# Layer 0's mixer in three-pass products: heads, gaps and forward heads on other engines, another order of products

## What is computed

```python
hl = modulate(x_lat, norm_g[l, 0], mod_l[0], mod_l[1])   # rms norm, gain, shift
hc = modulate(x_ctx, norm_g[l, 0], mod_c[0], mod_c[1])
aq, ak, av, ao, ag, bq, bk, bv = split_cols(h @ w_in, EVEN_SPLITS)
# mLSTM, 4 heads of 128, forward and backward in time:
dmat = where(tri, b[t] - b[s] + li[s], -inf);  m_t = maximum(inter, max(dmat))
w = exp(dmat - m_t);  s = (q @ k.T) * w
h = num / maximum(abs(den), exp(-m_t))            # forward h + backward h
mlstm = sigmoid(ao) * rms_norm(h, head_g)
# window attention, 8 heads of 64, 2 key heads, rope, a sink per head, over context and band
lat = concatenate([mlstm, b_lat]);  x = x + mod[2] * (lat @ w_out)
```

## Time and profile before

| | |
|---|---|
| median of 3 runs | 1662.94 us |
| the profiled execution, its span | 1663.01 us, 1661.7 us |
| PE busy | 1559.9 us, 94% |
| PEld, DVE, ACT, POOL busy | 78%, 70%, 44%, 29% |
| chain that ended last | PE 81%, DVE 9%, ACT 5% |
| heads of layer 0 (131.29 to 298.38) | 55.58, 55.58 and 55.93 us |
| head 0 ends | 131.29 us |

### The profile page before, as it was taken

How to read it: one execution, slowest core, us unless ns; L and a number is a source line. 1 busy time by engine, 2 the same in 40 slices (tenths; PEclk the granted TensorE clock), 3 DMA queues, 4 the chain that set the end, 5 groups by cost and what they waited for, 6 DMA issues and landing times.

```text
span 1661.7 us, 25035 instructions
## 1 busy us (share of the span) xinstructions
PE 1559.9 (94%) x9548; PEld 1298.8 (78%) x9548; DVE 1155.7 (70%) x2094; ACT 723.8 (44%) x1349; POOL 481.1 (29%) x385
## 2 busy tenths in 40 slices
PE   6999999989999999989898999998999999999888
PEld 5565566768888888866667999998888888898778
DVE  5467787869777797747767788666666666543764
ACT  2442434353333333344442655544444444454454
POOL 1012104102221110115430111025566656532652
PEclk9999999999999999999999999999999999999999
DMA  9223224314344466503234555553444434444240
GB/s 389 104 102 125 91 64 140 140 38 167 138 152 152 141 209 204 193 20 102 94 109 166 178 184 184 186 174 115 144 143 137 137 136 133 136 134 148 88 143 26
DMA packets 63943, 231.23 MB, mean 139 GB/s; under 512 B 7520, under 2 KB 8544, under 8 KB 63568
## 3 DMA queue, kind: packets, MB, share of 16 engines
q1 hardware_dynamic: 60912, 218.66, 38.7%
q0 software_dynamic: 2192, 6.29, 1.1%
q10 hardware_dynamic: 720, 4.68, 0.7%
HBM read 228.55 MB, written 1.05 MB: 138 GB/s over the span
## 4 chain that ended last, share of the span: by engine, by line
PE 81%; DVE 9%; ACT 5%; issue 3%; DMA 1%; POOL 1%; SPq 0%; ACTq 0%; DVEq 0%; POOLq 0%
PE ps L267 13%; PE ps L269 13%; PE ps L268 13%; PE ps L249 10%; PE ps L1314 4%; PE ps L1316 4%; PE ps L1315 4%; PE ps L257 2%; PE ps L742 2%; PE ps L732 2%; DVE big L687 2%; PE ps L635 1%; ACT big L668 1%; DMA ring<-in_ada_first 1%; DVE weights_rest L282 1%
## 5 line engine op out<-in xcount | busy, mean ns | idle before, releaser
L282 DVE TENSOR_TENSOR weights_rest<-ring,weights_rounded 128x1024 fp32r<-128x1024 f32 x192 | 267.4, 1394 | 69.8 <-ACT weights_rounded L276 69.5
L276 ACT ACTIVATE weights_rounded<-ring 128x1024 fp32r<-128x1024 f32 x233 | 244.3, 1053 | 119.7 <-PE ps L1316 94.1
L267 PE MATMUL ps<-h_hi,weights_rounded 128*128 128x512 f32 (+1 forms) x640 | 215.0, 336 | 0.0
L268 PE MATMUL ps<-h_lo,weights_rounded 128*128 128x512 f32 (+1 forms) x640 | 215.0, 336 | 0.0
L269 PE MATMUL ps<-h_hi,weights_rest 128*128 128x512 f32 (+1 forms) x640 | 215.0, 336 | 0.0
L1300 POOL TENSOR_TENSOR big<-scratch 128x512 f32<-128x512 f32 (+1 forms) x44 | 64.2, 1460 | 392.2 <-DVE scratch L1286 392.2
L288 POOL TENSOR_TENSOR weights_rest<-ring,weights_rounded 128x1024 fp32r<-128x1024 f32 x41 | 98.4, 2404 | 177.3 <-ACT weights_rounded L276 177.3
L1240 ACT ACTIVATE scratch<-ps,vectors 128x512 f32<-128x512 f32 (+1 forms) x88 | 59.1, 672 | 191.0 <-PE ps L269 182.2
L249 PE MATMUL ps<-h,ring 128*128 128x512 f32 x288 | 132.6, 617 | 2.2 <-DVE h L488 2.2
L269 PEld LDWEIGHTS ps<-h_hi,weights_rest 128*128 128x128 f32 x640 | 121.5, 190 | 12.6
L268 PEld LDWEIGHTS ps<-h_lo,weights_rounded 128*128 128x128 f32 x640 | 121.5, 190 | 12.5
(11 more groups left out here) (383 smaller groups left out, 3979.2 us busy)
## 6 DMA issues: line engine op xcount, KB each, us to landing
ring<-in_up SPq DMA_DIRECT2D x88, 512.0 KB, 3.8
ring<-in_ada_rest SPq DMA_DIRECT2D x80, 512.0 KB, 4.5
ring<-in_a_in SPq DMA_DIRECT2D x80, 512.0 KB, 3.5
ring<-in_down SPq DMA_DIRECT2D x44, 512.0 KB, 3.6
ring<-in_even SPq DMA_DIRECT2D x20, 512.0 KB, 4.2
ring<-in_ada_first SPq DMA_DIRECT2D x16, 512.0 KB, 9.0
ring<-in_wout SPq DMA_DIRECT2D x16, 512.0 KB, 3.6
ring<-in_odd SPq DMA_DIRECT2D x16, 512.0 KB, 3.7
```

What stands on the lines that cost most here:

```text
L267: te.matmul(bank[:, 0:n], wh[:, k, :], hi(k), start=k == 0, stop=False)
L268: te.matmul(bank[:, 0:n], wh[:, k, :], lo(k), start=False, stop=False)
L276: sc.activation(pair[0], place(*key), ACT.Copy).then_inc(*mark("rounded", *key))
L282: ve.tensor_tensor(pair[1], place(*key), pair[0].bitcast(F32), ALU.subtract).then_inc(*mark("rest", *key))
```

## The change

- The five products of each head and the three of even_pre are `pe_product3` products. ACT rounds each tile; the rests of tiles 0, 1 and 4 (of head 0 also 2) and of even_pre 1 and 2 are on POOL, the others on DVE. The tiles are released at the rest instead of the product. The output projection's first pairs continue the rotation of the slots.
- h is split: DVE scales 16 half blocks, ACT adds the shift and rounds, DVE subtracts. The three tiles of even_pre are rounded before the fourth group of rows is copied; the rows are turned between the products of ada_first; gates' and keys' products run block by block together, ahead of the values'.
- The values' products have the model dimension on the partitions; ACT copies them, TensorE transposes four blocks, ACT copies again.
- The gaps are on ACT, straight from the spread maxima in PSUM (Relu, bias, then Exp); MREP and its copies are gone. Each head's two spreads stand at the end of the head before, those of head 0 behind its product 2. GT holds the negative.
- The forward heads are on ACT (a copy with a scale from PSUM).
- DVE's adaptive tiles stand elsewhere in a head; in head 0 five of them stand between rope and decays. One tile moves from layer 1's heads to layer 1's output projection.

```diff
     for i in range(AH):
-        tile(("even", i, 0), "even", 5 * i, "product", "even", i, 0)
+        for s in range(3):
+            tile(("even", i, s), "even", 5 * i + s, even_rest(i, s), "even", i, s)
         ada_tiles(6 * i + 4, 6 * i + 5, 6 * i, 6 * i + 1)
...
-    ODD_ADA = [(68, 69), (70, 71), (72,), (73,)]
+    ODD_ADA = [(68, 69), (70,), (71,), (72,)]
+    WOUT1_ADA = [(73, 74), (75,), (76,), (77,), (78,), (79,), (), ()]
...
             if g == 3:
                 act_rsqrt((0, 0), TOK)
+                for x in range(3):
+                    act_round(("even_pre", x), PAIR_PRE[x], [])
...
+            if s in (8, 12, 15):
+                pe_rows(s // 4 - 2 + (s == 15))
...
+        for x, (k, s, cols) in enumerate(parts):
+            ve.scalar_tensor_tensor(FULL_EVEN[:, cols], xv[:, k, 256 * s:256 * s + 256], GAIN[:, s * KD + k:s * KD + k + 1],
+                                    RS[:, 256 * s:256 * s + 256], ALU.mult, ALU.mult).then_inc(*mark("scaled", "even", k, s))
+            if x >= 2:
+                rest(*parts[x - 2])
...
+    def pe_spread(i):
+
+        for dr in range(2):
+            te.wait_ge(*at("maxima", dr))
+            te.matmul(BANK[SPREAD[dr]], CT[0:4, C_SEL + 128 * i:C_SEL + 128 * i + 128], rows[6 + dr], start=True,
+                      stop=True).then_inc(*mark("maxima_spread", dr, i))
...
     def pe_even(i):
         us, E = sum(units0(i), []), ("even", i)
-        pe_product(("even", i, 0), BANK[6], TOK, hk(0, TOK))
+        pe_even_product(i, 0, BANK[6])
+        if i == 0:
+            pe_norm(KEY0, t1, BANK[1], TOK)
+            pe_even_turn(("even_pre", 2), VFM0[0], BANK[2])
+        pe_even_product(i, 1, BANK[7])
+        if i:
+            te.wait_ge(*at("mixed_heads", i - 1))
+        pe_norm(("even", i, 0), t1, BANK[5], TOK)
+        te.wait_ge(*at("aq_copied", i))
+        pe_even_product(i, 2, BANK[7])
         if i == 0:
             pe_gates()
...
+            te.wait_ge(*at("v_copied", 0))
             pe_spread(0)
...
+        te.wait_ge(*at("gaps", i, 0, *last_gap(0)))
...
-        pe_product(("even", i, 4), BANK[7], TOK, hk(0, TOK))
+        pe_even_turn(("even", i, 3), VFM0[1], BANK[6])
+        pe_even_product(i, 4, BANK[7])
...
+        if i + 1 < AH:
+            pe_spread(i + 1)
         te.wait_ge(*at("heads_normed", i))
...
         def gap_exps():
+            sc.wait_ge(*(at("numerators", i - 1, 3) if i else at("gates_copied")))
+            for dr, s, lo, n, pos, W in decays():
+                sc.wait_ge(*at("maxima_spread", dr, i))
+                c = 128 * s + 64 * dr + i
+                sc.activation(W, BANK[SPREAD[dr]][:, lo:lo + n], ACT.Relu,
+                              bias=GT[:, c:c + 1]).then_inc(*mark("gaps", i, dr, s, lo))
...
         sc.wait_ge(*at("product", "even", i, 3))
+        sc.wait_ge(*at("normed", "even", i, 0))
+        sc.activation(VFM0[1], BANK[6], ACT.Copy).then_inc(*mark("copied", "even", i, 3))
+        act_even_round(i + 1, 0)
+        sc.wait_ge(*at("turned", "even", i, 3))
         sc.activation(av3[:, :, 0:128], v3(BANK[6], 128), ACT.Copy).then_inc(*mark("av_copied", i))
...
         act_exps(us)
+        act_even_round(i + 1, 1)
         sc.wait_ge(*at("product", "even", i, 4))
...
+            if t:
+                forward_head(t - 1)
+        forward_head(3)
...
         dve_rope(E, ROPE1, BANK[5], t2, [] if i else [at("roped", *KEY0)])
-        dve_ada(6 * i + 2)
+        if i == 0:
+            ve.wait_ge(*at("cond_rows_act"))
+            dve_ada(4)
+            dve_ada(0)
+            dve_ada(2, 1)
...
+        pool_even_rest(i, 4)
+        pool_even_rest(i + 1, 0)
+        pool_even_rest(i + 1, 1)
```

More of the change, by code:

```diff
@@ L493, in build, with even_parts, act_even_h @@
-    K0, V0, MREP = BIG[:, 0:512], BIG[:, 512:1024], BIG[:, 1024:5120]
+    H_HI0, H_LO0 = rounded("h_even_hi", "h", 0, KD * TOK), rounded("h_even_lo", "big", 1024, KD * TOK)
+    FULL_EVEN = MIX
+    def even_parts():
+        for k in range(KD):
+            for s in range(2):
+                yield k, s, slice(k * TOK + 256 * s, k * TOK + 256 * s + 256)
+    def act_even_h():
+        for k, s, cols in even_parts():
+            sc.wait_ge(*at("scaled", "even", k, s))
+            sc.activation(H_HI0[:, cols], FULL_EVEN[:, cols], ACT.Identity,
+                          bias=mod(0, 0, s)[:, k:k + 1]).then_inc(*mark("h_rounded", "even", k, s))
+            if (k, s) == (4, 1):
+                act_even_round(0, 0)
+        act_even_round(0, 1)
@@ L494, in build @@
+    K0, V0 = BIG[:, 0:512], BIG[:, 512:1024]
     arow = BIG[:, 6144:6144 + 5120]
     rows = [arow[0:4, TOK * j:TOK * j + TOK] for j in (2, 3, 4, 5, 6, 7, 0, 1, 8, 9)]
+    rows[6:8] = [RS[0:4, TOK * j:TOK * j + TOK] for j in range(2)]
     GT, EM, MASK0 = SCR[:, 0:512], SCR[:, 512:544], SCR[:, 544:1568]
@@ L540, in act_pre @@
         act_square(KEY0, t1, BANK[0], TOK)
+        sc.wait_ge(*at("product", "even_pre", 2))
+        sc.activation(VFM0[0], BANK[2], ACT.Copy).then_inc(*mark("copied", "even_pre", 2))
+        act_even_round(0, 2)
         act_norm(KEY0, t1, BANK[1], TOK)
-        sc.wait_ge(*at("product", "even_pre", 2))
+        sc.wait_ge(*at("turned", "even_pre", 2))
         sc.activation(V0, BANK[2], ACT.Copy).then_inc(*mark("v_copied", 0))
-    def act_maxima(dr):
-        for h in range(AH):
-            x = AH * dr + h
-            sc.wait_ge(*at("maxima_spread", dr, h))
-            sc.activation(MREP[:, x * TOK:(x + 1) * TOK], BANK[SPREAD[x % 3]],
-                          ACT.Copy).then_inc(*mark("maxima_copied", dr, h))
     def act_floors():
@@ L604, in pool_pre @@
     def pool_pre():
+        for x in (1, 2):
+            pool_rest(("even_pre", x), PAIR_PRE[x], [])
         po.wait_ge(*at("square_sum", "x", KD - 1))
```

235 lines of the change are left out of this document (120 added, 115 removed).

## The result

The changed kernel took 1668.4 us, median of 14 runs, against 1663.0 for the kernel before on the same chip: ratio 1.0028, 95% interval 1.0019 to 1.0038. It is slower by 0.3%, where 1646.9 was forecast and 1654.5 was the range's upper end. The profiled execution has a span of 1666.5 us, which with 1.3 around it is 1667.8.

The account below looks back on a forecast made before the run. TensorE bounds a head up to S, an ACT and DVE chain its tail. Head 0 -1.7, heads 1 and 2 -8.4, head 3 -5.0, odd heads -2.4, projection +0.2, contention +1.2: -16.1, 1663.0 to 1646.9; range 1640 to 1654.5.

Parts of the forecast that it names:

- Products of 5.44, S 29 after the start: Layer 0's heads: three-pass products take 5.44 us; S, the end of attention scores, comes 6.0 earlier, 29.0 after head start.
- The tail of 22.4: From S to a head's end: 20.6 us as before, plus 1.8 for spreads.
- Contention: POOL's subtractions clear DVE's scalings by 3 us; smaller slowing costs +0.3 a head, 1.2 in all (bounds 0 and 4).
- The spreads, 1.8 on the path: Turn of the heads: two spreads of the maxima, 0.91 each, add 1.8 us behind the last weighing.
- The forward heads on ACT, 1.0 against 1.05: Head tails: DVE's cycle for one of four forward heads takes 1.0 us where it was 1.05.
- The last head's +1.0: Head 3: three roundings of the mixture on ACT ahead of its last two forward heads add 1.0 us.
- Head 0, -1.7: Opening and head 0: ends at 129.6 against 131.29, -1.7 us; parts placed by hand, +-3.
- Each tile's load is issued 3 us or more before its rounding: Weight ring: every three-pass weight is rounded well ahead, its load issued at least 3 us before.
- The opening: Before head 0: three roundings ahead of ACT's fourth row copy lose 1.6 us; rows turned at 37.9, products start at 41.0.
- The moved tile, -2.4 + 0.2: Adaptive tile moved from layer 1's heads to its output projection: -2.4 us in odd heads, +0.2 in the projection.
- Rival (a): The clock falls after each spread at the turn of heads; three heads lose 4.8 us: 1651.7, chance 0.18.
- Rival (c): POOL's three subtractions a head each hold an on-path DVE operation 2.14 us; twelve make 25.7: 1671.4, chance 0.03.

Follow-up runs that it names:

- spread_early: Changed kernel with the next head's two spreads moved on TensorE from behind the last weighing to behind the numerators; 1660.2 us, ratio 0.9957.
- opening_round: Changed kernel with ACT's rounding of head 0's third weight tile moved from inside the gate rows to behind the second tile's; 1666.0 us, ratio 1.0005.
- ada4_early: Changed kernel with head 0's first two adaptive tiles summed on DVE right behind the key's normalisation, not behind the rope; 1661.8 us, ratio 0.9968.
- rows_first: Changed kernel with ACT's three roundings of the first weight tiles behind the fourth copy of the shift and scale rows; 1670.3 us, ratio 1.0034.
- round_late: Changed kernel with ACT's rounding of the next head's second weight tile moved from behind the exponentials to behind the heads' norm; 1659.0 us, ratio 0.9956.
- forward_dve: Changed kernel with the four forward heads back on DVE, one scaling of 128x128 behind each inverse; 1663.6 us, ratio 0.9998.
- best_d: Changed kernel with ada4_early, opening_round, spreads behind the numerators, next heads' roundings re-placed and the last head's forward heads on DVE; 1643.5 us, ratio 0.9875.
- three_fixes: Changed kernel with the edits of ada4_early, round_late and spread_early together; 1651.2 us, ratio 0.9901.

## Why the prediction was wrong, step by step

- **Products of 5.44, S 29 after the start**: right, 29.1 in head 1 (139.53 to 168.66). The gain of 6.0 before S is real.
- **The tail of 22.4**: 24.4. The step that failed is "Contention", with its 1.2 us in all. It put POOL's subtraction at S + 8.2 to S + 10.7, and three paragraphs earlier stands the first denominator at S + 8.7; the trace has S + 8.4 and S + 8.85. But it asked only whether the *scalings* lay clear of POOL, since the earlier trace rows is about those. The operation that was hit is of 128x2. It was priced at 0.20 and took 1.87. Three heads: 5.
- **The spreads, 1.8 on the path**: right, 1.9 by spread_early.
- **The forward heads on ACT, 1.0 against 1.05**: 1.05 against 1.04, no matter.
- **The last head's +1.0**: 1.6 (7.55 against 5.93). 0.8 of it is the wait for ACT that was priced, 0.8 is POOL on the fourth floor, which was not.
- **Head 0, -1.7**: +8.2, the largest miss, and for the most part the same step. Four operations of DVE on the path ran beside a subtraction of POOL, none of them a scaling: the gains of the opening (1.53 against 0.24), the first copy of the gate rows (2.54 against 0.39; opening_round gave 2.1 back), the sixth adaptive tile (6.3 against 2.4) and the first floor (1.86 against 0.15). These are 1.3, 2.1, 3.9 and 1.7, or 9.0. The 3.9 is read from the trace, no run changes it alone. The gate rows were priced from the earlier trace rows, a time without POOL beside it.
- **"Each tile's load is issued 3 us or more before its rounding"**: wrong in head 0, where `dve_ada(4)` had moved behind the rope and the fifth weight tile takes that tile's place in the ring: load at 93.27, rounding at 96.74, ACT idle for 12.73. On the path it cost little, the 1.6 us for which the decays waited, since DVE's five tiles held them until 102.9 anyway. The 6.7 of ada4_early are more than this, because that edit also takes two of the five tiles out of the way. "From there DVE rules" was right.
- **The opening**: the turned rows came at 37.94, forecast 37.9. The products started 1.4 later than forecast, by the gains, and the order that the prediction charged with 1.6 is the better one (rows_first).
- **The moved tile, -2.4 + 0.2**: right, -2.47 and about 0.
- **Rival (a), the clock falls after each spread**: behind one of the three pairs of spreads here (243 to 249), one of ada4_early's (183 to 192), none of round_late's. It happens, but in heads without a spread ahead of them as well.
- **Rival (c), POOL holds DVE up, chance 0.03**: the mechanism is the one that happened. It named "a scaling or another operation of DVE that is on the path", at 2.14 each; it came once a head at 1.7, again in the last, and in the opening and head 0 besides, some 15 us in all.
- **What no term held**: 3.9 us in unchanged code, with the low clock.

The sum: head 0 is 9.9 over its forecast and heads 1 to 3 are 8.3 over (5 for the first floors, 0.8 for the fourth in the last head, perhaps 1.6 for the low clock at 243 and 291, the rest small), the end of the program 3.9, less 1.4 that the forecast held for contention and the projection: 20.7. The profiled execution took 1667.8 against 1646.9, which is 20.9. In head 0 the four operations and the waits are 10.6, so other parts placed by hand were 0.7 too long. Of the 21 us some 14 are contention beyond the 1.2 that was allowed for, about 4 lie in unchanged code with the low clock, and 1.6 are the late load.

## What to carry to other kernels

List the times at which GpSimd works, and hold them against *every* operation of VectorE on the path, tiny ones too: here the price was the time to the end of GpSimd's instruction, not a share of VectorE's own. When a consumer of a ring's tile is moved back, find the tile that takes its place, and see what stands in the queue behind that one's first use; do it for each head, not for the typical one. A long wait on an engine is not yet a loss: read on the engine that sets the pace how much of it arrives there (1.6 of 12.73 here). A repair of one wait can turn into contention, so take the waits away one by one and then together. And a gain of a few us in a kernel whose clock falls now and then is compared by stretches of the trace, since unchanged code differed by 4 us here.

## What the runs showed of the hardware

- A VectorE operation of 128x2 with both inputs in SBUF takes 0.15 us alone and 1.87 when GpSimd's subtraction of 128x1024 begins 0.5 ahead of it. Beside GpSimd's shorter subtractions of 128x512 (1.24 each) it took 0.33 (forward_dve, last head). The same holds for a copy of 4x512 (0.39 to 2.54) and for sums of 128x1024 (1.22 to 3.35). A reciprocal of 128x256 did not mind: 1.75 with a subtraction beside it (best_d, 121.37) and 1.75 without (changed kernel, 133.60). The Trainium skill (GPSIMD Engine Reference, Specifications) names as contended the VectorE instructions in a two-port mode or with two SBUF inputs. The trace agrees for the operations with two SBUF inputs and for the reciprocal, which has one; in which mode the copy ran, the trace does not show.
- The slowing is mutual: GpSimd's eight products of 128x128 took 3.45 us or 8.37. The Trainium skill (Perfetto Trace Analysis, GPSIMD Engine Instruction) warns that their spans don't compose and that the spacing of starts is to be used; by starts it is 3.41 and 8.34, so here the spans hold.
- The two spreads of a head, matmuls with 4 rows, take 1.98 us at a granted clock of 1.00 and 3.77 at the low one (head 0 of three_fixes).
